# One plain gate and up pair fewer, and T sums formed in place with their low parts added by DMA

## What is computed

```python
def rmsnorm(x, g):
    return x * lax.rsqrt(jnp.mean(x * x, axis=-1, keepdims=True) + EPS) * g

def conv_gated_mlp(h, w_gate, w_up, conv_ffn_w, conv_ffn_b, w_down):
    g = causal_dwconv(h @ w_gate, conv_ffn_w, conv_ffn_b)   # 3 taps along the tokens
    return (jax.nn.gelu(g) * (h @ w_up)) @ w_down           # 2048 -> 6144 -> 2048

x = x + rmsnorm(hybrid_mixer(rmsnorm(x, norm_mix_pre), ...), norm_mix_post)
x = x + rmsnorm(conv_gated_mlp(rmsnorm(x, norm_ffn_pre), ...), norm_ffn_post)
```

## Time and profile before

| | us |
|---|---|
| median of 3 runs | 2139.85 (2139.79 to 2140.06) |
| time of the profiled execution | 2136.76 |
| its span, first to last instruction | 2134.9 |
| TensorE busy | 2117.7 (99%) |
| VectorE, ScalarE, GpSimd busy | 1681.4 (79%), 1023.1 (48%), 351.3 (16%) |

### The profile page before, as it was taken

How to read it: one execution, slowest core, us unless ns; L and a number is a source line. 1 busy time by engine, 2 the same in 40 slices (tenths; PEclk the granted TensorE clock), 3 DMA queues, 4 the chain that set the end, 5 groups by cost and what they waited for, 6 DMA issues and landing times.

```text
span 2134.9 us, 44301 instructions
## 1 busy us (share of the span) xinstructions
PE 2117.7 (99%) x18238; PEld 2086.4 (98%) x18238; DVE 1681.4 (79%) x2297; ACT 1023.1 (48%) x1297; POOL 351.3 (16%) x444
## 2 busy tenths in 40 slices
PE   9999999999999999999999999999999999999998
PEld 8999999999999999999999999999999999999997
DVE  7777767777855887888888888888887867767876
ACT  6555554456322554444444444444454545445543
POOL 1222223222100001111111111111211101012002
PEclk9999999999999999999999999999999999999999
DMA  5788988988543446888888888787889648679645
GB/s 178 161 195 202 213 191 191 211 185 193 158 129 99 153 122 181 225 218 219 212 218 220 219 218 219 217 222 217 236 215 283 188 159 286 178 189 280 203 139 188
DMA packets 239138, 423.32 MB, mean 198 GB/s; under 512 B 17264, under 2 KB 152304, under 8 KB 237696
## 3 DMA queue, kind: packets, MB, share of 16 engines
q0 software_dynamic: 88608, 159.44, 36.3%
q1 hardware_dynamic: 147776, 256.84, 36.1%
q10 hardware_dynamic: 2592, 4.72, 0.6%
HBM read 382.12 MB, written 89.16 MB: 221 GB/s over the span
## 4 chain that ended last, share of the span: by engine, by line
PE 96%; DVE 1%; ACT 1%; issue 1%; POOL 1%; POOLq 0%; DVEq 0%; ACTq 0%
PE bank L2110 30%; PE bank L2112 30%; PE bank L2111 30%; PE bank L2497 2%; PE bank L2189 1%; PE bank L2202 1%; PE bank L2214 0%; PE bank L2213 0%; PE bank L2229 0%; ACT w_all L782 0%; ACT act_hi L1164 0%; PE bank L2277 0%; DVE w_all L1246 0%; PE bank L2166 0%; POOL act_lo_f L773 0%
## 5 line engine op out<-in xcount | busy, mean ns | idle before, releaser
L2110 PE MATMUL bank<-act_hi,w_all 128*128 128x256 f32 x3272 | 909.9, 278 | 3.8 <-DVE up L1974 1.4
L2112 PE MATMUL bank<-act_hi,w_all 128*128 128x256 f32 x3272 | 903.7, 276 | 0.0
L2111 PE MATMUL bank<-act_lo,w_all 128*128 128x256 f32 x3272 | 903.6, 276 | 0.0
L2110 PEld LDWEIGHTS bank<-act_hi,w_all 128*128 128x128 f32 x3272 | 614.3, 188 | 11.2 <-issue 5.7
L2111 PEld LDWEIGHTS bank<-act_lo,w_all 128*128 128x128 f32 x3272 | 614.4, 188 | 0.4 <-issue 0.2
L2112 PEld LDWEIGHTS bank<-act_hi,w_all 128*128 128x128 f32 x3272 | 614.3, 188 | 0.0
L2110 PE MATMUL bank<-tsum,w_all 128*128 128x256 f32 x1280 | 353.5, 276 | 0.0
L2112 PE MATMUL bank<-tsum,w_all 128*128 128x256 f32 x1280 | 353.3, 276 | 0.0
L2111 PE MATMUL bank<-tsum,w_all 128*128 128x256 f32 x1280 | 353.3, 276 | 0.0
L1158 ACT ACTIVATE w_all<-raw_s 128x1024 fp32r<-128x1024 f32 x172 | 182.6, 1062 | 244.1 <-PE bank L2112 224.5
L1246 DVE TENSOR_TENSOR w_all<-raw,w_all 128x1024 fp32r<-128x1024 f32 x134 | 164.0, 1224 | 147.2 <-ACT w_all L782 145.0
(11 more groups left out here) (404 smaller groups left out, 3523.5 us busy)
## 6 DMA issues: line engine op xcount, KB each, us to landing
raw<-weights SPq DMA_DIRECT2D x262, 512.0 KB, 4.5
w_sums<-weights POOLq DMA_DIRECT2D x96, 512.0 KB, 7.1
raw_s<-weights SPq DMA_DIRECT2D x84, 512.0 KB, 5.8
raw_s<-weights POOLq DMA_DIRECT2D x84, 512.0 KB, 5.8
raw_a<-weights SPq DMA_DIRECT2D x66, 512.0 KB, 5.3
raw_s<-w_sums SPq DMA_DIRECT2D x48, 512.0 KB, 5.3
t_spill<-h_out POOLq DMA_DIRECT2D x48, 256.0 KB, 3.7
act_lo_f<-t_spill POOLq DMA_DIRECT2D x11, 1024.0 KB, 9.4
```

The costliest lines, as they stand in the source:

```text
L2110: pe.matmul(dst, ah, bh, start=start, stop=False, skip_group_check=goes_on)
L2111: pe.matmul(dst, ah, bl, start=False, stop=False, skip_group_check=goes_on)
L2112: return pe.matmul(dst, al, bh, start=False, stop=stop, skip_group_check=goes_on)
```

## The change

`PLAIN` goes from 6 to 5, so one pair moves from the plain to the fast form. With it:

- `t_form` writes its four results over the quadrants of x1 that it has read (T1, T2, T3, T0 in the order of the quadrants) and no longer into `sq`; all three steps after the first wait for the one before them.
- `t_hi` copies the high part as before, and copies once more with a scale of -1 into the low part's place: ScalarE does two copies for each tile k. `t_lo` is gone from VectorE. In its place GpSimd issues two accumulating DMAs for each k (`add_t`), 256 KB each, that add the sums in x1 onto the negated high parts.
- The tiles are taken in `T_ORDER`. Three semaphores `lows_added` (`T_PART`: the first two tiles, the next four, the last two) take the place of `t_formed` and `t_split`: SyncE's first loads into `raw_s1`, `raw_s3`, `raw_a22`, the first copy into `w_2`, the first `form_s2` and TensorE's first product with a T operand wait for them.
- The square of the norm's denominator goes from VectorE to ScalarE. The first pair of the fast part takes `lo(0, 0)` ahead of `form_s2(0)`, and `t3_of_pair(1)` stands ahead of both.
- Banks of the last additions are renumbered, since the number of blocks is now odd.

```diff
-PLAIN = 6
+PLAIN = 5
+T_ORDER = (0, 1, 4, 5, 6, 7, 2, 3)
+T_PART = (0, 0, 1, 1, 1, 1, 2, 2)
...
+        def t_lows(eng, part):
+
+            eng.wait_ge(lows_added[part], 32 * T_PART.count(part))
...
+            def add_t(i):
+
+                k = T_ORDER[i]
+                pool.wait_ge(t_neg_done, i + 1)
+                for r in range(2):
+                    pool.dma_start(tsum[:, 2 * r:2 * r + 2, 1, k], in_two(x1[:, k + UK * r]).bitcast(F32R),
+                                   accum_op=ALU.add).then_inc(lows_added[T_PART[i]], 16)
...
+                formed = x1[:, k::UK].rearrange("p a (b n) -> p a b n", n=HS)
+                hi, lo = [tsum[:, :, part, k].rearrange("p (a b) n -> p a b n", b=2) for part in range(2)]
+                act.activation(hi, formed, ACT.Copy)
+                act.activation(lo, formed, ACT.Copy, scale=-1.0).then_inc(t_neg_done, 1)
...
-                chain(dve.tensor_tensor(t_f32[:, 1], b11, b12, ALU.subtract))
-                dve.tensor_tensor(t_f32[:, 2], b22, b12, ALU.subtract)
+                chain(dve.tensor_tensor(b11, b11, b12, ALU.subtract))
+                chain(dve.tensor_tensor(b12, b22, b12, ALU.subtract))
...
-            form_s2(0)
             lo(0, 0)
+            form_s2(0)
...
-                    pe.wait_ge(t_split, UK)
+                    for part in range(3):
+                        t_lows(pe, part)
```

More of the change, by code:

```diff
@@ L348, in block_kernel @@
         t_landed = [sem(f"t_landed{n}") for n in range(7)]
+        lows_added = [sem(f"lows_added{n}") for n in range(3)]
         y_stored = [sem(f"y_stored{n}") for n in range(2)]
@@ L401, in block_kernel @@
         P00, P01, P10, P11 = [act_quadrant(r, n) for r in range(2) for n in range(2)]
-        T0, T1, T2, T3 = [t_slot(t) for t in range(4)]
+        T1, T2, T3, T0 = [t_slot(t) for t in range(4)]
         OPERANDS = ((P00, T0, T1, T2, P10, P11, T3), (P01, P00, T0, T1, T2, P10, P11), (T3, P01, P00, T0, T1, T2, P10),
@@ L734, in add_to_s3 @@
                 pool.dma_start(raw_s3[:], weights[U_FF + 4 * (PLAIN + i)], accum_op=ALU.add).then_inc(s3_landed, 16)
-            for j in range(PLAIN - 2):
-                store_after(j)
+            def add_t(i):
[4 more added lines that the diff above has]
+                                   accum_op=ALU.add).then_inc(lows_added[T_PART[i]], 16)
+            for i in range(3):
+                add_t(i)
+            store_after(0)
+            store_after(1)
+            add_t(3)
+            store_after(2)
+            add_t(4)
+            add_t(5)
             add_to_s1(0)
+            store_after(3)
+            add_t(6)
+            add_t(7)
             add_to_s3(0)
-            store_after(PLAIN - 2)
             add_to_s1(1)
@@ L1834, in _ @@
             t_form(0)
-            t_lo(0)
             t_form(1)
@@ L1842, in _ @@
             taps(0)
-            t_lo(1)
+            t_form(2)
             gate_in(1, PT[0], open_used(1, 0))
-            t_form(2)
             split(N_FF + 14, 0)
@@ L1848, in _ @@
             t_after(0)
-            t_lo(2)
+            t_form(3)
             taps(1)
@@ L1859, in _ @@
             t_after(2)
-            t_form(3)
+            t_form(4)
             taps(3)
             split(N_FF + 17, 1)
-            t_lo(3)
+            t_form(5)
             up_tile(3, SB[2], open_used(3, 1))
             t_after(3)
-            t_form(4)
+            t_form(6)
             split(N_FF + 18, 0)
-            t_lo(4)
-            t_form(5)
+            t_form(7)
             split(N_FF + 19, 1)
-            t_lo(5)
-            gate_in(4, PJ[0], open_used(4, 0))
-            t_form(6)
-            taps(4)
-            split(N_FF + 20, 0)
-            t_lo(6)
-            t_form(7)
-            up_tile(4, PJ[1], open_used(4, 1))
-            t_after(4)
-            split(N_FF + 21, 1)
-            t_lo(7)
-            dve.scalar_tensor_tensor(out=acc[:], in0=acc[:], scalar=EPS * D / P, in1=acc[:], op0=ALU.mult, op1=ALU.mult)
-            split(N_FF + 22, 0)
-            split(N_FF + 23, 1)
+            t3_of_pair(1)
             def product_lo(i, n):
@@ L2059, in _ @@
                 if i == 0:
-                    up_tile(PLAIN - 1, PT[1], N_FAST)
+                    up_tile(PLAIN - 1, PJ[1], N_FAST)
                 elif i <= NS:
                     fast_h(j - 1, i - 1)
-                if i <= NS:
+                if 0 < i <= NS:
                     t_after(j - 1)
```

93 lines of the change are left out of this document (41 added, 52 removed).

## The result

The changed kernel takes 2151.98 us (median of 4 runs, 2149.64 to 2154.74), the kernel before 2139.82 in the same comparison: a ratio of 1.006, 95% interval 1.0047 to 1.0072. It is 12.2 us slower; I had forecast 8.9.

The account below looks back on a forecast made before the run. The prediction took TensorE's matmuls to bound the kernel. Gain -2.7, late second product +10.3 and clock +1.3 summed to +8.9 us, so 2139.85 became 2148.7 us, range 2137 to 2153.

Parts of the forecast that it names:

- One sign: Expected in the profile after: TensorE's longest wait, about 7 us, on VectorE's low part of S2.
- The gain: On TensorE: one pair goes from 192 matmuls to 168, taking off 2.7 us.
- The splits: Plain units 17 and 18: VectorE's low parts come 0.8 us late each, together 1.7 us on TensorE's path.
- the 10.3: Delay in us of the second product, starting at 834.6 instead of 824.33; it holds the 1.7 of the splits.
- Product 0: First fast product: about 1 us late, since t3_of_pair(1) waits for a store behind S1's addition.
- The queues: DMA queues q0 and q1: 12.8 and 5.4 us of transfers, 18.2 from 813.0, land the last low part at 831.2.
- the loads don't compete: Rival, 20%: q0's 12.8 us alone decide, last low part at 825.8, second product 5 to 5.5 us late; 2142.6 us.
- The dear addition: Rival, 10%: adding SBUF onto SBUF takes 3.3 us per transfer, five cost 9.2 us more; 2157.9 us.
- S2 to product 1: From the last low part's landing at 831.2, forming and splitting S2, to the second product's start at 834.6.
- The clock: TensorE behind the 7 us gap: 2.6 us at half rate cost 1.3 us; bounds 0 and 2.7.
- Behind it: After the second product's wait: nothing is short, and TensorE has no new wait from the third product on.
- the forecast's own case: Whole kernel: 2148.7 us, within 2144.2 to 2153, given 48%.

Follow-up runs that it names:

- e_order: Changed kernel with the splits of plain units 17 (ScalarE) and 18 (VectorE) moved ahead of T work; 2149.73 us, ratio 1.005.
- e_t3_back: Changed kernel with t3_of_pair(1) moved behind the low part of product 0 on VectorE; 2153.34 us, ratio 1.0063.
- e_copy: Changed kernel with its sixteen adding transfers made plain copies, leaving that part of the computation out; 2148.09 us, ratio 1.0045.
- e_six: Changed kernel with six plain pairs instead of five and the first S1 addition behind the last adding transfers; 2141.82 us, ratio 1.0012.
- e_best_4: Changed kernel with VectorE forming the last four T tiles' low parts, splits of units 17 and 18 ahead of T work, t3_of_pair(1) behind S2's sum; 2137.98 us.

## Why the prediction was right, and where it was short

The range and the sign held, and the place: the longest wait on S2's low part, behind the last DMA into `tsum`, the clock behind it, no new wait among the fast pairs. One sign did not come: TensorE was to stand still for about 7 us in one piece, and it stood still for 3.0 us ahead of product 0 and for 4.7 ahead of product 1. By its steps:

- **The gain**, -2.7: as worked out; all of it lies in the 12.2.
- **The splits**, 0.8 each: 1.2 and 0.9 us, 2.2 in all with a small third. They were counted within the 10.3, and they lie there; the traces of `e_order` show them getting there by way of the queue.
- **Product 0**, about 1 us late: its own wait was 3.0 us, for the store that `t3_of_pair(1)` waits for. It didn't matter for product 1, as `e_t3_back` shows.
- **The queues**, the last low part at 831.2: S2 started on it at 833.86, less the 1.7 of shift 832.1. The sum of engine time on both queues was 0.9 short in 18.2. The addition onto S1 was issued at 815.03, less the shift 1.8 us later than the 811.5 that I had put; the sum starts at 813.0 and doesn't see it. The case in which the loads don't compete (825.8) is out: both queues hold about half each where both have work, from 824 to 828 us in the changed kernel:

```profile
q0 software_dynamic: 300, 0.82, 54.7%
q1 hardware_dynamic: 222, 0.78, 47.8%
```

  That agrees with the Trainium skill's turn-taking (DMA: Bandwidth & Descriptors, section Queues, rings and completion order). The dear addition is out as well, at 3.3 us a transfer; from 828 to 830 us 256 KB take 1.3 us, near the 1.46 taken from the accumulating stores. The transfers took 3.8 to 13.4 us from issue to landing:

```profile
DMA to landing us min/median/max: 3.8/8.1/13.4
```

  But the sum was right as a total and not as a queue. It would have given 2.2 us for the stores moved away, and the run gave 1.2.
- **S2 to product 1**, 3.4 us: it took 4.0. Of the 0.6, 0.2 is an error in adding up: 1.22, 1.06, 1.22 and 0.1 are 3.6, as I had it elsewhere. The two taps (1.5 us) stand ahead of the low part on VectorE and end 0.3 to 0.4 us after ScalarE's high part; I had left them out. With the 0.9 and the 0.6 and roundings, product 1 was 11.9 us late and not 10.3.
- **The clock**, 1.3 us: 3.0. This is the step that failed most. It was sized by the program's start, as 2.6 us at half rate behind the gap. In fact TensorE ran at the lower level for 6.0 us behind the gap, and 3.0 us is over my upper bound too (one product, 2.7). The earlier low stretch over product 0 isn't the reason: the clock was back at the upper level from 833.6 us and fell again at 837.0, within the gap. In `e_copy`, where product 0 runs at the full rate, the clock falls only in the wait ahead of product 1, and it stays low for 5.5 us behind that product's start (834.48):

```profile
826.00:833.10 7.10, 2.98 (x24) 2.81 (x24) 3.46 (x4) 2.02 (x3) 0.00 (x0) 1.00 1.27 302
833.20:840.00 6.80, 5.52 (x26) 5.55 (x27) 3.40 (x3) 1.80 (x3) 1.45 (x2) 0.50 0.82 210
```

  In the six kernels in which the clock was low when product 1 began behind a wait, it stayed low for 4.4 to 6.0 us more, where the term had 2.6, and the way from product 1 to the last gate was 2.2 to 3.0 us longer.
- **Behind it**: "no new wait" held for the fast pairs. The 0.9 us in the down stage (L1969) was not seen. That wait is 0.5 to 0.6 us in the three profiles with six plain pairs (the kernel before, twice, and `e_six`) and 1.1 to 1.9 us in all eleven with five, `e_best_4` among them (1.4). So it goes with the number of plain pairs (43 fast pairs in place of 42, and the banks renumbered for it) and not with the T sums; by what way was not tried. It takes back a third of the 2.7 us that the change is for.

The chances: the forecast's own case came true, near its upper end.

## What to carry to other kernels

Work that moves from a busy engine to the DMA queues is free only while other work lies over the queues' end: here four plain units more or less decide between 2142 and 2152 us. Price such a move by the time for which all the DMA engines are full, across queues, with an adding transfer at twice a copying one; and do the last tiles, those that something waits for, on the engine. Where a wait on TensorE's path can't be avoided, matmuls that nothing reads keep its clock: by the traces they gave back the 3.0 us here (2.6 by the medians, whose intervals overlap).

## What the runs showed of the hardware

- An adding transfer within SBUF takes 1.9 times a copying one with the same 1 KB rows: 203 against 380 packets a microsecond on 16 busy engines. GpSimd's issue of two of them takes 2.4 us, and of two copying ones 1.4.
- Rows of 1 KB alone are hardly a brake: 0.37 MB a microsecond there, and 0.40 MB with the packets of loads and stores, most of them of 4 KB (824 to 828 us).
- At the half clock TensorE's matmuls stay evenly spaced, 0.213 us for 0.113; a trace shows it in the distances before any wait is read. The granted clock is to be read in stretches cut where it changes: over 10 us it reads 0.68 or 0.81, a mean of 0.5 and 1.0.
- Within one wait of 5 us the granted clock rose to 1.00 and fell to 0.50 again (the changed kernel, 833.6 to 837.0 us).
